# Even layer: squares and root earlier; odd gates and odd projection: another order of the same instructions

## The reference

```python
# even layer
oa = gla_chunked(aq, ak, av, log_a)                       # 4 heads of 128
oa = rmsnorm_2(oa, gla_gain) * silu(a_gate)
ob = swa_attention(bq, bk, bv, sinks, rel_bias) * silu(b_gate)
h  = h + concatenate([oa, ob]) @ w_out_even
# odd layer
cq, ck, cv, c_gate = split(rmsnorm_2(h) @ w_in_odd)
oc = moba_attention(cq, ck, cv, rel_bias)                 # 8 heads of 128
h  = h + (oc * silu(c_gate)) @ w_out_odd
```

## Time and profile before

| | us |
|---|---|
| median of 3 runs | 980.28 |
| lowest and highest | 979.52, 981.07 |
| the profiled execution's own time | 975.78 |
| its span (first to last instruction) | 974.0 |
| TensorE busy | 927.8 (95%) |
| VectorE busy | 707.0 (73%) |
| ScalarE busy | 534.6 (55%) |
| POOL busy | 304.2 (31%) |
| granted TensorE clock, mean over the span | 0.974 |

### The profile page before, as it was taken

One profiled execution on the slowest core, in us unless ns is written; L12 is line 12 of the kernel. 1 busy time (PEld: TensorE's weight loads), 2 busy tenths in 40 slices (PEclk: granted clock), 3 DMA queues, 4 the chain that ended last, 5 costly groups with the idle time before them and its releaser, 6 DMA issues.

```text
span 974.0 us, 19442 instructions
## 1 busy us (share of the span) xinstructions
PE 927.8 (95%) x6866; PEld 865.1 (89%) x6866; DVE 707.0 (73%) x1134; ACT 534.6 (55%) x914; POOL 304.2 (31%) x272
## 2 busy tenths in 40 slices
PE   5988989899999999999979999999999999998996
PEld 5977557799999999988969999999999879898995
DVE  3997679778888777888986797555556873475764
ACT  3465656566665444555634566654444772664645
POOL 1952020138885011120051288741110000330012
PEclk9799999999999999999979999999999998999998
DMA  8856185168888778789638986555666332255421
GB/s 330 303 199 215 50 236 186 46 225 273 290 275 279 279 261 283 249 318 311 231 75 212 263 285 211 182 187 172 191 189 192 112 109 87 87 174 181 166 87 44
DMA packets 57268, 195.90 MB, mean 201 GB/s; under 512 B 6407, under 2 KB 10007, under 8 KB 56952
## 3 DMA queue, kind: packets, MB, share of 16 engines
q1 hardware_dynamic: 55528, 192.66, 60.2%
q0 software_dynamic: 1680, 2.44, 1.1%
HBM read 192.59 MB, written 1.44 MB: 199 GB/s over the span
## 4 chain that ended last, share of the span: by engine, by line
PE 76%; DVE 15%; issue 4%; ACT 3%; DMA 1%; DVEq 0%; POOL 0%; SPq 0%; ACTq 0%
PE bank L534 23%; PE bank L535 22%; PE bank L536 22%; DVE w_lo L1564 3%; DVE ada_raw L1571 2%; ACT w_hi L1141 1%; DVE products L1666 1%; PE bank L632 1%; PE bank L923 1%; PE bank L949 1%; DVE ada_raw L1666 1%; DMA x<-x_in 1%; PE bank L877 1%; DVE ada_more L1666 1%; DVE ada_raw L1579 1%
## 5 line engine op out<-in xcount | busy, mean ns | idle before, releaser
L1564 DVE TENSOR_TENSOR w_lo<-raw,w_hi 128x1024 fp32r<-128x1024 f32 (+1 forms) x261 | 338.5, 1298 | 99.5 <-ACT w_hi L1141 96.6
L1141 ACT ACTIVATE w_hi<-raw 128x1024 fp32r<-128x1024 f32 (+1 forms) x261 | 272.1, 1044 | 174.1 <-PE bank L536 163.8
L534 PE MATMUL bank<-act_hi,w_hi 128*128 128x258 f32 (+1 forms) x872 | 248.9, 285 | 0.0
L535 PE MATMUL bank<-act_lo,w_hi 128*128 128x258 f32 (+1 forms) x872 | 246.6, 283 | 0.0
L536 PE MATMUL bank<-act_hi,w_lo 128*128 128x258 f32 (+1 forms) x872 | 246.3, 282 | 0.0
L534 PEld LDWEIGHTS bank<-act_hi,w_hi 128*128 128x128 f32 x872 | 165.9, 190 | 2.4 <-issue 1.9
L535 PEld LDWEIGHTS bank<-act_lo,w_hi 128*128 128x128 f32 x872 | 166.0, 190 | 0.1
L536 PEld LDWEIGHTS bank<-act_hi,w_lo 128*128 128x128 f32 x872 | 166.0, 190 | 0.0
L534 PE MATMUL bank<-hid_hi,w_hi 128*128 128x256 f32 x512 | 143.9, 281 | 0.0
L535 PE MATMUL bank<-hid_lo,w_hi 128*128 128x256 f32 x512 | 143.9, 281 | 0.0
L536 PE MATMUL bank<-hid_hi,w_lo 128*128 128x256 f32 x512 | 143.9, 281 | 0.0
(11 more groups left out here) (353 smaller groups left out, 1801.0 us busy)
## 6 DMA issues: line engine op xcount, KB each, us to landing
raw<-weights SPq DMA_DIRECT2D x247, 512.0 KB, 4.2
ada_raw<-ada SPq DMA_DIRECT2D x88, 512.0 KB, 5.2
raw<-weights SPq DMA_DIRECT2D x14, 384.0 KB, 4.5
ada_more<-ada SPq DMA_DIRECT2D x8, 512.0 KB, 5.4
bias<-bias_by_distance SPq DMA_DIRECT2D x8, 256.0 KB, 6.8
x<-x_in SPq DMA_DIRECT2D x1, 1024.0 KB, 7.4
ctx<-ctx_in SPq DMA_DIRECT2D x1, 1024.0 KB, 9.4
out<-result SPq DMA_DIRECT2D x4, 256.0 KB, 2.7
```

The costliest lines, as they stand in the source:

```text
L534: pe.matmul(dst, w[0], a[0], start=start, stop=False)
L535: pe.matmul(dst, w[0], a[1], start=False, stop=False)
L1141: act.activation(w_hi[:, slot, 0:width_of(c)], raw[:, slot, 0:width_of(c)], ACT.Copy).then_inc(weight_hi, 1)
L1564: dve.tensor_tensor(w_lo[:, slot, 0:w], raw[:, slot, 0:w], w_hi[:, slot, 0:w].bitcast(fp32), ALU.subtract).then_inc(weight_lo, 1)
```

## The change

ScalarE, even gates: the four squares go ahead of the conversion of step 4; the root goes from step 6 to step 5, and VectorE's reciprocal with it. ScalarE, odd gates: the conversion goes ahead of the eviction wait and the Silu. TensorE, odd projection: group 3 is left out of the steps k = 5, 6 and 7 and does these three behind them, ahead of group 4. ScalarE, odd projection: the root of one column goes from ahead of the loop to step 5, behind that step's `convert` (which, beyond the last chunk, does nothing) and ahead of its square.

```diff
@@ -1107,10 +1107,11 @@
             beat_turn(blocks, 7, prob_o)
             block_values(6)
             late("odd_out", odd_o, range(2, 4), range(4, 5))
-            late("odd_out", odd_o, range(4), range(5, 6), a_wait=odd_o_wait)
+            late("odd_out", odd_o, range(3), range(5, 6), a_wait=odd_o_wait)
             block_values(7)
-            late("odd_out", odd_o, range(4), range(6, 7), a_wait=odd_o_wait)
-            late("odd_out", odd_o, range(4), range(7, 8), a_wait=odd_o_wait)
+            late("odd_out", odd_o, range(3), range(6, 7), a_wait=odd_o_wait)
+            late("odd_out", odd_o, range(3), range(7, 8), a_wait=odd_o_wait)
+            late("odd_out", odd_o, range(3, 4), range(5, 8))
             late("odd_out", odd_o, range(4, 8))
             pe.wait_ge(square_sums, 6 * (KT - 2))
             for tt in range(2):
@@ -1484,6 +1485,11 @@
                 act.activation(gate[:, (g + 4) % 8, :], gate[:, (g + 4) % 8, :], ACT.Silu).then_inc(gated, 1)
 
             for g in range(8):
+                if g == 4:
+                    for h in range(4):
+                        act.wait_ge(g_o, 4)
+                        act.activation(sq[:, h, :], bank[4 + h % 2][:, (h // 2) * S:(h // 2 + 1) * S],
+                                       ACT.Square).then_inc(g_squared, 1)
                 convert(chunk0["even_g"] + g + 4)
                 if g == 0:
                     window_beat(9)
@@ -1493,12 +1499,9 @@
                 if g == 4:
                     for i in range(4):
                         gate_silu(i)
-                    for h in range(4):
-                        act.wait_ge(g_o, 4)
-                        act.activation(sq[:, h, :], bank[4 + h % 2][:, (h // 2) * S:(h // 2 + 1) * S],
-                                       ACT.Square).then_inc(g_squared, 1)
+                if g == 5:
+                    root(rms_gla[:], bank[6][0:H, 0:P], P, g_sums, 1, g_std)
                 if g == 6:
-                    root(rms_gla[:], bank[6][0:H, 0:P], P, g_sums, 1, g_std)
                     for h in range(4):
                         split(split0["even_o"] + h, oe_hi[:, h, :])
             for g in range(4, 8):
@@ -1511,9 +1514,9 @@
 
             norm(5, by_token=True)
             for g in range(8):
+                convert(chunk0["odd_g"] + g + 4)
                 act.wait_ge(evacuated, group0["odd_g"] + g + 1)
                 act.activation(gate_o[:, g, :], gate_o[:, g, :], ACT.Silu).then_inc(gated, 1)
-                convert(chunk0["odd_g"] + g + 4)
             for g in range(2):
                 convert(chunk0["odd_k"] + g + 4)
             convert(chunk0["odd_v"] + 4)
@@ -1534,9 +1537,10 @@
                     block_beat(g - 1)
             for b in (7, 8, 9):
                 block_beat(b)
-            act.activation(std[:, S:S + 1], eps[:], ACT.Sqrt)
             for g in range(KT):
                 convert(chunk0["odd_out"] + g + 4)
+                if g == 5:
+                    act.activation(std[:, S:S + 1], eps[:], ACT.Sqrt)
                 square_residual("odd_out", g)
                 act.activation(result[:, g, :], x[:, g, :], ACT.Copy, scale=V("final_gain", g, 1)).then_inc(raw_hi, 1)
             act.wait_ge(sums_ready, 8)
@@ -2045,7 +2049,7 @@
                             dve.scalar_tensor_tensor(state[:, n, 1, :], state[:, n - 1, 1, :],
                                                      decay[:, 1, 1, n:n + 1], kv[:, 1, :], ALU.mult,
                                                      ALU.add).then_inc(g_state, 1)
-                if g == 6:
+                if g == 5:
                     dve.wait_ge(g_std, 1)
                     dve.reciprocal(rms_gla[:], rms_gla[:]).then_inc(g_rstd, 1)
             dve.wait_ge(gated, 8 + 8)
```

## The result

The changed kernel took 973.83 us (median of 14 runs) beside 978.50 for the kernel before (median of 14, the three known ones among them). The two medians are 4.7 us apart (0.9952). One of the 14 runs before took 1810.93 us and doesn't count; over the others the ratio of the runs is 0.9941, with 95% between 0.9925 and 0.9956: 5.8 us faster, 4.3 to 7.3. On the 980.28 of the prediction that ratio gives 974.5, the forecast; on the 978.5 measured beside it, 972.7, or 0.2 under the low end of the range. The level from which the prediction counted, a median of three runs, lies 1.8 above that of the 14, which is more than the 0.7 that its range left for scatter. Sign and size of the gain hold. How the size comes about doesn't, in one of its four terms.

A forecast was written before the change was run, and what follows sets the result against it. TensorE, holding 76% of the chain, was taken to bound the kernel, so its waits counted. Terms 2.4+0.8+2.2+0.35 = 5.75 us took the profiled 975.78 to 970.0; with 4.5 carried over to the runs, 974.5 us, range 972.9 to 977.0.

The forecast's parts named there:

- Even waits, 2.4: Even gates: TensorE's waits before the column sums (1.41) and before the spread (1.02) vanish, saving 2.4 us.
- rival 2: Even projection: last Silus, products and oe_lo come late and TensorE waits about 1.2 us; 975.7 or 976.5; chance 0.10.
- a drain: Even gates, ScalarE: about 1.38 us besides the table load; tile 7 would come about 1.4 us late.
- Odd gates, 2.2: Before the odd values: TensorE's wait for ck_o's eviction falls from 2.73 to 0.55, saving 2.2 us.
- rival 3: Odd gates: VectorE stays behind and the 2.7 us wait remains, or a third is gained; 976.7; chance 0.06.
- Odd projection, 0.35: Odd projection: the last head's values and the chain to group 4 start 0.35 us sooner; ends 0 and 0.7.
- The clock, 0.8: Start of the even projection, behind the spread: less half-rate time, saving 0.8 us; ends 0 and 1.7.
- Rivals 4 and 5: 4: even gain waited away at the norm, odd too, 980, chance 0.05; 5: clock slows groups 6 and 7, 983.9, 0.02.
- The sign that the prediction named for being wrong: TensorE: a half-rate stretch longer than 3.4 us, one of three signs that would make the forecast wrong.

The follow-up runs named there:

- experiment 5: The kernel before, unedited, profiled a second time; 980.63 us.
- 1 even part: The kernel before with only the squares, root and reciprocal of the even gates moved; 975.77 us against 979.63, 0.9959.
- 6 squares: The kernel before with only the four squares moved ahead of the conversion, root and reciprocal left at step 6; 972.39 us, one run.
- 8 before, 128 rows: The kernel before with only the spread's tile made 128 rows, rows 8 to 127 zero; 979.37 us against 979.88, 0.9997.
- 3 projection: The kernel before with only the odd projection's part: group 3 held back, one-column root moved to step 5; 980.61 us against 979.63, 1.0002.
- 4 hold: The kernel before with only group 3 held back in the odd projection, the one-column root left ahead of the loop; 979.63 us, one run.
- 9 banks swapped: The kernel before with only the banks of the odd values swapped, (7, 3) for (3, 7); 976.49 us against 979.44, 0.9969.
- 2 odd gates: The kernel before with only the conversion moved ahead of the Silu in the odd gates; 975.90 us against 979.63, 0.9959.
- 10 (changed again): The changed kernel, unedited, run again; 973.22 us against 979.44 for the kernel before, 0.9939.
- 7 changed, 128 rows: The changed kernel with the spread's tile made 128 rows, rows 8 to 127 zero; 972.81 us, 0.9934 of the kernel before.
- 11 everything: The changed kernel with the spread's tile of 128 rows and the banks of the odd values swapped; 969.12 us against 979.44 for the kernel before, 0.991.
- 12 values sooner: As 11 everything, with the last head's values ahead of step k=5 in the odd projection; 968.20 us against 979.44 for the kernel before, 0.9896.

## Why the prediction was right or wrong

**What the medians hide and the lengths show.** Runs of one kernel differ by several us, so parts worth one or two can't be read from medians of this many runs. The trace allows a closer reading: lengths between two fixed instructions of TensorE. Stage A runs from the spread (L1058) to the last of the odd norm's sums (L624); stage B from there to the first final sum (L1117 or L1118). The ends of stage B in before, b0 (experiment 5) and the changed kernel:

```profile
870.02 0.36 PE L624 MATMUL bank<-mean,sq 128*128 128x1 f32 x2
...
965.01 0.50 PE L1117 MATMUL bank<-mean,square_sum 128*128 128x1 f32 x4
```

```profile
872.96 0.36 PE L624 MATMUL bank<-mean,sq 128*128 128x1 f32 x2
...
969.87 0.50 PE L1117 MATMUL bank<-mean,square_sum 128*128 128x1 f32 x4
```

```profile
870.24 0.36 PE L624 MATMUL bank<-mean,sq 128*128 128x1 f32 x2
```

With 963.14 from above the three are 94.99, 96.91 and 92.90. All profiles, taken the same way:

| kernel | stage A | half rate in A | stage B | `ck_o` wait | half rate in B |
|---|---|---|---|---|---|
| before | 31.03 | 3.4 us | 94.99 | 2.7 | none |
| 5 (before again) | 32.43 | 6.8 | 96.91 | 2.7 | 3.4 |
| 1 even part | 30.88 | 3.4 | 96.51 | 2.7 | 3.4 |
| 6 squares | 29.52 | none | 96.92 | 2.7 | 3.4 |
| 8 before, 128 rows | 29.53 | none | 96.41 | 2.7 | 3.4 |
| 3 projection | 30.99 | 3.4 | 96.14 | 2.7 | 3.4 |
| 4 hold | 30.89 | 3.4 | 96.13 | 2.7 | 3.4 |
| 9 banks swapped | 29.52 | none | 93.51 | 1.2 | none |
| 2 odd gates | 30.93 | 3.4 | 92.86 | 0.6 | none |
| changed | 30.93 | 3.4 | 92.90 | 0.6 | none |
| 10 (changed again) | 31.15 | 3.4 | 92.50 | 0.6 | none |
| 7 changed, 128 rows | 29.78 | none | 92.90 | 0.6 | none |
| 11 everything | 29.77 | none | 91.65 | none | none |
| 12 values sooner | 29.77 | none | 90.76 | none | none |

**Even waits, 2.4: right.** Squares, sums, root and reciprocal fell where the steps put them, both waits went, and experiments 1 and 6 show that the two moves are worth their own waits, 1.4 and 1.0. One step of it was off, without harm in the profile of the changed kernel: POOL took 4.52 for its four `oe_lo`, not the 3.78 of the earlier trace rows, so tile 3 is ready later than reckoned. The reason is on record, and it is the change itself. Before, VectorE made its reciprocal while POOL began; now the reciprocal is done and a `w_lo` runs there, and the first subtraction takes twice as long (the first two lines are of the changed kernel, the third of the kernel before):

```profile
837.74 1.23 DVE L1568 TENSOR_TENSOR w_lo<-raw,w_hi 128x1024 fp32r<-128x1024 f32 x1 [0.73 <-ACT w_hi L1142]
838.08 1.47 POOL L2121 TENSOR_TENSOR oe_lo<-tile_f,oe_hi 128x256 fp32r<-128x256 f32 x1 [2.48 <-ACT oe_hi L1147]
```

```profile
838.35 0.72 POOL L2117 TENSOR_TENSOR oe_lo<-tile_f,oe_hi 128x256 fp32r<-128x256 f32 x1 [6.60 <-ACT oe_hi L1146]
```

The fourth runs beside the next `w_lo` in both orders, and takes 1.72 in both. The four took 4.51 or 4.52 in all six profiles with the root moved and 3.76 to 3.78 in the other eight. In the changed kernel the last three matmuls ahead of k=3 run at half rate, and these cover it, so TensorE waits for no `oe_lo`; with the clock full in that place the cover is gone, and experiments 7, 11 and 12 pay 0.4 there. That is a small piece of rival 2, and it has nothing to do with a drain.

**Odd gates, 2.2: right by the wait, too small by the time.** The wait fell by 2.12, and VectorE was not behind, so rival 3 falls.

**Odd projection, 0.35: right.** `oo_lo` at 0.73 and `w_lo` at 0.77 were forecast at 0.9 each, and two waits of 0.9 would have left only 0.06 of the 1.86 saved. The prediction's own terms give what was measured: 0.41 and 0.35 of lost cover are 0.76, and 1.45 less six more matmuls (not nine: three of them stood behind k=7 before) is 0.75. Stage B of experiments 3 and 4 is 0.37 shorter than that of 1 (96.51 less 96.14). The one-column root's place costs TensorE nothing on either side: it delays the sixth square, and ScalarE's idle time before the seventh falls from 1.90 to 0.81.

**The clock, 0.8: the step that failed.** The prediction put it at the spread: "The change takes the idling from in front of the spread and leaves the 16 matmuls", and it expected the stretch of the earlier trace rows to go in part. In both profiles of the changed kernel it is there in full, and stage A is as long as before (30.93 against 31.03): the term of 0.8 measured nothing. Experiment 8 takes the two suspects apart: with the idle 1.02 left in and 128 rows instead of 8 the stretch is gone. That is one profile, and two with 8 rows lack the stretch as well, so the count has to decide. Over all profiles the stretch stood behind 8-row matmuls in 8 of 10 and behind 128-row ones in 0 of 4; were the rows indifferent, chance would give such a split in some 1.5 of 100. With 8 rows it stood in 5 of 7 with the idling in front and in 3 of 3 without. So the rows most likely matter and the idling in front of them was not needed; by the table, the price of a stretch is 31.0 less 29.5, or 1.5 us. Experiments 6 and 9 have the 8 rows, the idle time and no stretch: it is a matter of most executions, not of all.

The clock's gain came at a place that the prediction costed at nothing: the odd values. The first profile has a wait of 2.73 there and full rate behind it, and I took this for the kernel's behaviour. It was the exception. Of the 7 profiles that have the wait of 2.7, 6 show 3.4 us at half rate behind it; behind a wait of 1.23, 0.6 or none, it is in 0 of 7 (chance would give that in 0.2 of 100). Experiment 9 shortens the wait in another way, with the Silus and conversions in their old order, and the stretch does not come either, so it hangs on the wait and not on ScalarE's order. The price comes out the same three times, two of them against the one profile without the stretch: 96.51 or 96.41 less 94.99 is 1.5 or 1.4; and in experiment 9, 96.5 less 93.51 is 3.0 = 1.5 of wait and 1.5 of clock. The timed gain of that one was 3.0 too. In experiment 2 the same sum is 2.1+1.5 = 3.6, inside its 2.5 to 5.4, where the wait alone is outside. The granted clock of the timed runs points the same way, no more: its mean was 0.9739 in experiment 9 and 0.9737 in experiment 2, against 0.9727 in the kernel before beside each; 3.4 us at half rate in 6 of 7 executions would make 0.0015, and these means have standard errors of 0.0003 to 0.0008.

**The whole.** 2.4+2.1+0.36 of waits and 1.5 x 6/7 = 1.3 of clock at the odd values give 6.2 us, inside the 4.3 to 7.3 measured; the forecast's 5.75 is inside as well, with one term in the wrong place. That 0.8 stood near the 1.3 is luck. The parts timed alone add up to 4.0+4.0-0.2 = 7.8, each with 1.4 to 2.5 of doubt, so no interplay can be read from them. That the profiled pair shows only 1.9 has three reasons: the 2.8 us that the changed kernel's profile lost ahead of the column sums (see the profile after); stage B of the first profile, which is 1.5 short of its kind for want of the stretch, so that the pair shows no gain of clock at all; and 0.4 from the last 96 matmuls. These, at 113.3 ns a step in the first profile, took 117.8 in that of the changed kernel, and 113.4 in experiment 10, the same program. Of 14 profiles ten show the lower value, and experiments 5, 6, 7 and the changed kernel the higher: an execution's luck. Like against like, stage B went from 96.51 (experiment 1, odd stages unchanged) to 92.50 (experiment 10), both at the lower step: 4.0 us, 2.5 of waits and 1.5 of clock.

**Rivals 4 and 5** fall: nothing waits again at the norm (stage A unchanged), and groups 6 and 7 ran at full rate. The sign that the prediction named for being wrong, a half-rate stretch longer than 3.4 us, does stand in the changed kernel's profile (10.2 us from 818.2), but ahead of the column sums, where the kernel before had 6.8 and the earlier trace rows shows 4 of them.

**What stays open.** What the stretch behind the spread is worth in timed runs: by the table 1.5 us, yet experiment 8 found 0.9997 with an interval that only just holds 0.9985, its mean granted clock is that of the kernel before beside it (0.9739 and 0.9737), and 7 is no faster than the changed kernel by its interval. Against that, 11 took 4.1 us less than 10 beside it, where the table has 1.4 in stage A and 0.9 in stage B; the intervals of their two ratios overlap, so that is a hint and no price. Whether 12 beats 11 is not settled by its time; the trace has stage B 0.9 shorter. Why the clock falls in most executions and not in all was not tried.

## What to carry to other kernels

One profile is one execution. Where a price hangs on the clock, look at a TensorE wait of this length as though the half-rate stretch stood behind it, even if this profile shows full rate there: shortening the wait of 2.7 was worth 2.1, and 1.5 more where the stretch came. To read parts of one or two us in a kernel whose runs scatter by several, compare lengths between two fixed instructions of the bound engine over many profiles. And when two suspects stand together ahead of a slow stretch, as idle time and matmuls of few rows did here, change the one that costs nothing (here zero rows) before pricing the other.

## What was not expected of the hardware

- Sixteen 128-column matmuls with 8 rows were followed by half rate in 8 of 10 profiles, the same with 128 rows, of which 120 are zeros, in 0 of 4; they took 2.05 and 1.95 us.
- A pause of TensorE of 2.7 us in dense work, ahead of the odd values, was followed by half rate in 6 of 7 profiles, one of 1.23 us or less, or none, in 0 of 7.
- The same 96 matmuls in the same program ran at 113.4 or 117.8 ns a step, in different executions, with the granted clock at 1.00 in both.
- A POOL subtraction of 128x256 took 0.72 us where no `w_lo` of VectorE's (128x1024) ran beside it and 1.47 or 1.72 where one did, so moving a reciprocal of VectorE's made the four `oe_lo` 0.74 longer (4.52, not 3.78).
